# A masked softmax over compressed keys: sixteen small passes on the vector engine made into four wide ones

## The reference, cut to what matters

```python
valid_c = cmp_end[None, :] <= t[:, None]          # cmp_end = 16*c + 31
s_c = einsum('bqgrd,bcgd->bgrqc', qb, k_cmp) * scale + dense_bias(t[:, None] - cmp_end[None, :])
p_c = softmax(where(valid_c, s_c, NEG)) * any(valid_c)
o_c = einsum('bgrqc,bcgd->bqgrd', p_c, v_cmp)      # added with its gate to the other two branches
```

## Time and profile before

| | us |
|---|---|
| median of 3 runs | 2486.55 (2485.26 to 2487.08) |
| the profiled execution | 2487.18 |
| its span on the core | 2485.4 |
| around the span | 1.8 |
| PE busy | 2435.1 |
| DVE busy | 1407.3 |
| ACT busy | 974.9 |
| POOL busy | 177.5 |

### The profile page before, as it was taken

How to read it: one execution, slowest core, us unless ns; L and a number is a source line. 1 busy time by engine, 2 the same in 40 slices (tenths; PEclk the granted TensorE clock), 3 DMA queues, 4 the chain that set the end, 5 groups by cost and what they waited for, 6 DMA issues and landing times.

```text
span 2485.4 us, 31282 instructions
## 1 busy us (share of the span) xinstructions
PE 2435.1 (98%) x12006; PEld 2033.1 (82%) x12006; DVE 1407.3 (57%) x2914; ACT 974.9 (39%) x1808; POOL 177.5 (7%) x245
## 2 busy tenths in 40 slices
PE   9999999999999989999999999999999998999998
PEld 7888889888887878778888888878878887888887
DVE  6435456676666676675443446667644566643444
ACT  4223234432335565553222234555423345422232
POOL 0000000101002221220000000222200002000000
PEclk9999999999999999999999999999999999999999
DMA  4454443233321111113223234211112431223222
GB/s 152 110 130 132 105 138 125 98 107 110 102 85 52 60 52 60 52 60 102 93 92 107 94 102 126 70 58 53 59 63 92 135 119 68 93 83 110 96 86 92
DMA packets 86382, 231.36 MB, mean 93 GB/s; under 512 B 8489, under 2 KB 23465, under 8 KB 86235
## 3 DMA queue, kind: packets, MB, share of 16 engines
q1 hardware_dynamic: 81072, 221.42, 27.2%
q10 hardware_dynamic: 5162, 7.95, 2.1%
HBM read 217.79 MB, written 11.53 MB: 92 GB/s over the span
## 4 chain that ended last, share of the span: by engine, by line
PE 90%; DVE 5%; ACT 3%; issue 2%; DMA 0%; POOL 0%; DVEq 0%; SPq 0%; ACTq 0%
PE bank L975 88%; PE bank L1188 1%; ACT t_pp L1634 1%; DVE t_pp L2142 1%; DVE t_PS L1894 0%; ACT t_whi L1481 0%; ACT t_tmp L1481 0%; ACT t_PS L1481 0%; DVE t_wlo L1889 0%; ACT t_pw L1634 0%; PE bank L1362 0%; DVE t_pw L2142 0%; DVE t_ST L2409 0%; DVE t_CB L2006 0%; DVE t_QS L2235 0%
## 5 line engine op out<-in xcount | busy, mean ns | idle before, releaser
L975 PE MATMUL bank<-t_XH,t_whi 128*128 128x512 f32 x2064 | 813.5, 394 | 6.5 <-DVE t_sa L2142 3.5
L975 PE MATMUL bank<-t_XH,t_wlo 128*128 128x512 f32 x2064 | 804.7, 390 | 0.0
L975 PE MATMUL bank<-t_XL,t_whi 128*128 128x512 f32 x2064 | 804.3, 390 | 0.0
L1889 DVE TENSOR_TENSOR t_wlo<-t_raw,t_whi 128x1024 fp32r<-128x1024 f32 (+2 forms) x418 | 479.4, 1149 | 363.1 <-ACT t_whi L1481 360.1
L1481 ACT ACTIVATE t_whi<-t_raw 128x1024 fp32r<-128x1024 f32 (+3 forms) x422 | 415.7, 988 | 416.8 <-PE bank L975 363.4
L975 PEld LDWEIGHTS bank<-t_XH,t_whi 128*128 128x128 f32 x2064 | 388.2, 188 | 89.5 <-DVE t_sa L2142 4.7
L975 PEld LDWEIGHTS bank<-t_XH,t_wlo 128*128 128x128 f32 x2064 | 387.9, 188 | 82.1
L975 PEld LDWEIGHTS bank<-t_XL,t_whi 128*128 128x128 f32 x2064 | 388.4, 188 | 77.2
L975 PE MATMUL bank<-t_RX,t_whi 128*128 128x512 f32 x1056 | 325.1, 389 | 0.0
L2006 DVE TENSOR_TENSOR t_tmp<-bank,t_RB 128x512 f32<-128x512 f32 x178 | 122.5, 688 | 222.6 <-PE bank L975 217.5
L975 PEld LDWEIGHTS bank<-t_RX,t_whi 128*128 128x128 f32 x1056 | 198.2, 188 | 41.1
(11 more groups left out here) (322 smaller groups left out, 2747.5 us busy)
## 6 DMA issues: line engine op xcount, KB each, us to landing
t_raw<-in_f_in SPq DMA_DIRECT2D x86, 512.0 KB, 3.2
t_raw<-in_f_out SPq DMA_DIRECT2D x32, 384.0 KB, 3.0
t_raw<-in_w_conv SPq DMA_DIRECT2D x24, 512.0 KB, 3.2
t_raw<-in_w_merge SPq DMA_DIRECT2D x24, 512.0 KB, 3.2
t_raw<-in_fg SPq DMA_DIRECT2D x22, 512.0 KB, 3.2
t_raw<-in_fu SPq DMA_DIRECT2D x22, 512.0 KB, 3.2
t_raw<-in_f_out SPq DMA_DIRECT2D x32, 320.0 KB, 3.0
t_raw<-in_w_g SPq DMA_DIRECT2D x16, 512.0 KB, 3.2
```

The source lines that it names most:

```text
L975: return e.matmul(o, l, r, start=start, stop=stop, skip_group_check=True)
L1889: e.tensor_tensor(wlo[n % NRAW][:, 0:width], raw[n % NRAW][:, 0:width], f32(whi[n % NHI][:, 0:width]), ALU.subtract).then_inc(*w_lo.tick(n))
```

## The change

The mask moves to ACT: its copy of cscore's bank becomes four instructions, one per token block, of the function Identity with a bias that is a column of the constants: 1e30 on the partitions (keys) past that block's last key. The table is added in the bank, in place, still block by block; minimum, subtraction, exponential, sum, reciprocal, gate and product are then made once per group for all 16 pairs of block and head by 32 keys. The bank is now freed by the subtraction. POOL's one clearing of t_PC falls away.

```diff
-C_ID, C_INV, C_SEL, C_C1024, C_C256, C_ANY, C_END = 0, 128, 256, 258, 259, 260, 261
+C_ID, C_INV, C_SEL, C_C1024, C_C256, C_ANY, C_LATE, C_END = 0, 128, 256, 258, 259, 260, 261, 265
+    for i in range(4):
+        c[:, C_LATE + i] = np.where(np.arange(P) % 32 >= 8 * i + 7, BIG, 0.0)
...
-                     (2, 0): {0: one("cnorm", g, 0), 1: one("cnorm", g, 1), 2: one("cnorm", g, 2), 3: one("cnorm", g, 3)},
+                     (2, 0): {0: one("cnorm", g, 0), 1: one("cnorm", g, 1), 2: one("cnorm", g, 2)},
...
(ACT)
-            copy(T[4], banks[("cscore", g)]).then_inc(*copied.tick(("ct", g), ("free", ("cscore", g))))
+            for i in range(4):
+                c = slice(i * P, (i + 1) * P)
+                e.activation(T[4][:, c], banks[("cscore", g)][:, c], ACT.Identity, bias=cst[:, C_LATE + i:C_LATE + i + 1]).then_inc(
+                    *copied.tick(("ct", g), ("free", ("cscore", g))))
 
         def csoft(g, i):
-            n = 8 * i + 7
-            sc = T[4][:, i * P:i * P + 4 * n]
-            on.wait_ge(*calc.at(("csub", g, i)))
-            e.activation(sc, sc, ACT.Exp, scale=-1.0).then_inc(*curve.tick(("cexp", g, i)))
+            if i == 3:
+                on.wait_ge(*calc.at(("csub", g)))
+                e.activation(T[4], T[4], ACT.Exp, scale=-1.0).then_inc(*curve.tick(("cexp", g)))
...
(DVE, csoft)
-            e.tensor_tensor(sc, ps, TB4[:, :, c0:c0 + 16 * (n - 1) + 1:16], ALU.add).then_inc(
-                    *evac.tick(("cs", g, i), ("free", ("cback", g))))
-            on.wait_ge(*evac.at(("cs", g, i)))
-            e.tensor_reduce(csm[:, i, 0, :], sc, AX.X, ALU.min).then_inc(*calc.tick(("cmin", g, i)))
-            on.wait_ge(*calc.at(("cmin", g, i)))
-            e.tensor_tensor(sc, sc, csm[:, i, 0, :].unsqueeze(2).to_broadcast([P, 4, n]), ALU.subtract).then_inc(
-                *calc.tick(("csub", g, i)))
+            e.tensor_tensor(ps, ps, TB4[:, :, c0:c0 + 16 * (n - 1) + 1:16], ALU.add).then_inc(*evac.tick(("cs", g, i)))
+            if i == 3:
+                on.wait_ge(*evac.at(("cs", g, 3)))
+                e.tensor_reduce(csum(0), heads16(banks[("cback", g)]), AX.X, ALU.min).then_inc(*calc.tick(("cmin", g)))
+                on.wait_ge(*calc.at(("cmin", g)))
+                e.tensor_tensor(heads16(T[4]), heads16(banks[("cback", g)]), csum(0).unsqueeze(2).to_broadcast([P, 16, 32]),
+                                ALU.subtract).then_inc(*calc.tick(("csub", g), ("free", ("cback", g))))
...
(DVE, cnorm: reduce, reciprocal, gate and product per block i before; now)
+            if i == 0:
+                on.wait_ge(*curve.at(("cexp", g)))
+                e.tensor_reduce(csum(1), heads16(T[4]), AX.X, ALU.add).then_inc(*calc.tick(("csum", g)))
+            if i == 1:
+                on.wait_ge(*calc.at(("csum", g)))
+                e.reciprocal(csum(2), csum(1)).then_inc(*calc.tick(("crec", g)))
...
+                e.tensor_tensor(csm[:, 3, :, :], csm[:, 2, :, :], gn[:, :, 12 * g:12 * g + 12:3], ALU.mult).then_inc(
+                    *calc.tick(("cgate", g)))
+            if i == 2:
...
+                e.tensor_tensor(heads16(PC.rearrange("p i c -> p (i c)")), heads16(T[4]), csum(3).unsqueeze(2).to_broadcast([P, 16, 32]),
+                                ALU.mult).then_inc(*calc.tick(("pcw", g)))
...
(POOL, sparsezero)
-            e.memset(f32(VC[1]), 0.0)
-            e.memset(PC, 0.0).then_inc(*cleared.tick("sparse"))
+            e.memset(f32(VC[1]), 0.0).then_inc(*cleared.tick("sparse"))
```

More of the change, by code:

```diff
@@ L2279, in svs, with heads16, csum @@
                     low_scaled(lo, src, norm_r(1)[0][:, i:i + 1], hi, ("sv", half, i), ("free", ("sv", half, i)))
-        def cpart(i):
-            return 8 * i + 7, T[4][:, i * P:i * P + 4 * (8 * i + 7)].rearrange("p (r c) -> p r c", r=4)
+        def heads16(x):
+            return x.rearrange("p (h c) -> p h c", h=16)
+        def csum(k):
+            return csm[:, k, :, :].rearrange("p i r -> p (i r)")
         def csoft(g, i):
-            n, sc = cpart(i)
+            n = 8 * i + 7
             if i == 0:
@@ L2300, in cnorm @@
-        def cnorm(g, i):
-            n, sc = cpart(i)
-            on.wait_ge(*curve.at(("cexp", g, i)))
-            e.tensor_reduce(csm[:, i, 1, :], sc, AX.X, ALU.add).then_inc(*calc.tick(("csum", g, i)))
-            on.wait_ge(*calc.at(("csum", g, i)))
-            e.reciprocal(csm[:, i, 2, :], csm[:, i, 1, :]).then_inc(*calc.tick(("crec", g, i)))
-            on.wait_ge(*calc.at(("gn",)))
-            on.wait_ge(*calc.at(("crec", g, i)))
-            e.tensor_tensor(csm[:, i, 3, :], csm[:, i, 2, :], gn[:, i, 12 * g:12 * g + 12:3], ALU.mult).then_inc(
-                *calc.tick(("cgate", g, i)))
-            on.wait_ge(*cleared.at("sparse"))
-            if g:
-                on.wait_ge(*full.at(("cturn", g - 1)))
-            on.wait_ge(*calc.at(("cgate", g, i)))
-            e.tensor_tensor(PC[:, i, :].rearrange("p (r c) -> p r c", r=4)[:, :, 0:n], sc,
-                            csm[:, i, 3, :].unsqueeze(2).to_broadcast([P, 4, n]), ALU.mult).then_inc(*calc.tick(("pcw", g)))
+            e.tensor_tensor(ps, ps, TB4[:, :, c0:c0 + 16 * (n - 1) + 1:16], ALU.add).then_inc(*evac.tick(("cs", g, i)))
@@ new lines, in csoft @@
+            if i == 3:
[4 more added lines that the diff above has]
+                                ALU.subtract).then_inc(*calc.tick(("csub", g), ("free", ("cback", g))))
+        def cnorm(g, i):
+            if i == 0:
[4 more added lines that the diff above has]
+                e.reciprocal(csum(2), csum(1)).then_inc(*calc.tick(("crec", g)))
+                on.wait_ge(*calc.at(("gn",)))
+                on.wait_ge(*calc.at(("crec", g)))
+                e.tensor_tensor(csm[:, 3, :, :], csm[:, 2, :, :], gn[:, :, 12 * g:12 * g + 12:3], ALU.mult).then_inc(
+                    *calc.tick(("cgate", g)))
+            if i == 2:
+                on.wait_ge(*cleared.at("sparse"))
+                if g:
+                    on.wait_ge(*full.at(("cturn", g - 1)))
+                on.wait_ge(*calc.at(("cgate", g)))
+                e.tensor_tensor(heads16(PC.rearrange("p i c -> p (i c)")), heads16(T[4]), csum(3).unsqueeze(2).to_broadcast([P, 16, 32]),
+                                ALU.mult).then_inc(*calc.tick(("pcw", g)))
```

## The result

The changed kernel takes 2480.18 us (median of 16 runs, 2478.63 to 2482.25) against 2486.01 us for the kernel before (16 runs, 2483.14 to 2489.09). The ratio is 0.9976, with an interval of 0.997 to 0.9983: 5.8 us less, between 4.2 and 7.5. The kernel is faster, and the difference is clear of the noise, where the forecast gave 0.77 to no change that can be told.

What follows compares the result with a forecast made beforehand. PE, busy 98% of the span, was taken as the bound, so only its waits on DVE or ACT could return. Terms +1.2 - 3.2 + 0.5 - 0.2 - 0.9 - 0.2 = -2.8 us gave 2483.7 us, range 2480.2 to 2487.0.

Steps and rivals of the forecast that it cites:

- the cover given to cnorm: cnorm blocks 1 and 2: hidden by `values` and dense items, nothing gained; block 0 -0.2, block 3 of group 3 -0.9.
- The mask: ACT's four copies before cback add 0.59 us each time, fully paid in groups 0 and 3; sum +1.2 us.
- csoft, blocks 0 and 1: DVE work ahead of `weigh` shrinks: groups 0 to 3 give -1.2, -0.5, -1.0, -0.5; sum -3.2 us.
- block 3: Wide minimum and subtraction add 0.9 us ahead of `weigh` of tile 3, paid only in group 2: +0.5 us.
- `weigh` of tile 3: Group 1, cnorm's head: this `weigh` comes earlier by what DVE gained, an estimated -0.2 us.
- still heads before PE takes it: The held bank, freed 1.4 us later by the change, would still be free heads before PE needs it.
- A dense item gives DVE 5.4 us to catch up, so whatever it does under one is free: Under dense items, 756 to 1084 us: DVE work costs nothing; only small items ahead of `weigh` are paid for.
- In the csoft heads no wait of PE over 0.3 us: Expected sign: no longer PE waits there, except about half a microsecond after block 3 of group 2.
- 1.4 us lost: Group 0: cscore's eight matmuls took 3.50 us at low clock against group 3's 2.08; nothing put in the sum.
- Rival 3: ACT reloads its table around each cscore: 8 loads, 10.3 us, giving +7.5 us, 2494; chance 0.03.
- Rival 1: Gain hidden or paid back, since shorter `weigh` waits uncover `rest`: about 0, 2486 to 2487 us; chance 0.16.
- Rival 2: DVE's catching up dissolves more of PE's `weigh` waits: -5 to -8 us, 2478.5 to 2481.5; chance 0.19.

Runs made afterwards that it cites:

- no mask: Changed kernel with ACT's four masked copies as one plain copy of 512 columns, mask left out; 2477.84 us, ratio 0.9962.
- csoft only: Changed kernel with cnorm block by block as in the kernel before; 2485.9 us, ratio 0.9994.
- bank held: Changed kernel with cback's bank returned to PE's ring two tiles later, at cnorm 2 instead of cnorm 0; 2482.28 us, ratio 0.9981.
- extra at tile 1: Changed kernel with a second, identical sum on DVE (0.68 us) at tile 1 of head (2,0), in all four groups; 2483.81 us, one execution.
- late cback: Changed kernel with cback one tile later and the adds of blocks 0 and 1 sharing tile 1; 2477.39 us, ratio 0.996.
- cnorm only: Kernel before with the wide cnorm alone, csoft per block on a 32-column grid, no mask; 2482.55 us, ratio 0.9984.
- late adds: late cback with block 1's add moved to tile 2 beside block 2's; 2476.24 us, ratio 0.9959.
- late minimum: late cback with minimum, subtraction and exponential moved to tile 0 of head (2,0) and cnorm's three steps one tile later; 2482.41 us, ratio 0.9984.
- before again: Kernel before, unchanged, one more profiled execution; 2489.03 us.

## Why the prediction was wrong, step by step

The step that failed is the cover given to cnorm: it put the saving in blocks 1 and 2 at nothing, and all of cnorm in group 2. The runs show 0.95 us in group 2 and 0.4 more than forecast in group 3. The terms one by one:

**The mask, +1.2 us.** Right in size and place: 0.55 in group 3, 0.56 between cscore and cback in group 0, 0.1 together in the others ("no mask").

**csoft, blocks 0 and 1, -3.2, and block 3, +0.5.** In group 1 the forecast had -0.5 and -0.2 for `weigh` of tile 3, and 0.89 came. In group 3 it had -0.5 with the mask's +0.59, and "csoft only" has +0.05: right. In group 0 all terms together were -0.7, and 0.6 to 0.8 came, which can't be told apart from more or less, since group 0 moves by 1.2 to 1.4 us by itself. In group 2 it had -1.0 + 0.5, and -0.95 came: if blocks 0 and 1 gave their 1.0, block 3 gave nothing back. No run separates the two. The statement that the held bank would be free "still heads before PE takes it" was false. PE took it at 981.79 and waited 0.67 us, but "bank held" shows the price of that wait as nothing.

**cnorm.** "Blocks 1 and 2 are covered, by `values` and dense items" is the step that failed. cnorm in group 2 was forecast at 0 and gave 0.95; group 3 was forecast at -1.0 and gave 1.39. In group 2 DVE runs without a pause from csoft to the dense item, so that what is saved in cnorm's tiles arrives at the end as far as PE can follow. In group 3 a dense item does lie behind, but it brings DVE work of its own and waits for ACT, and 0.43 of 0.68 us added before it come out behind it ("extra at tile 1"). "A dense item gives DVE 5.4 us to catch up, so whatever it does under one is free" counted the item's length on PE, and not DVE's share in it.

**What made me take it for covered** was in group 2 PE's list of waits. I took its rows for the sum of what can come back. In group 2 it shows 0.16 us of wait where 0.53 us lie between two starts, against 0.21 when DVE is early, and it fell by 0.3 where 1.87 came back. In group 3 the list did show the waits that went, and the fault was to count the cover as free.

**The signs.** PE's 1.15 us before 1082.78 is gone, as said. "In the csoft heads no wait of PE over 0.3 us" failed: waits of 0.43 to 0.52 us for `rest` (t_PS) are left in groups 0, 2 and 3, and of 0.36 for `weigh` in group 1. PE's wait before cback of group 0 was to be 1.9 and is 3.30; the row of 1.30 from which that came was short because cscore ran slowly.

**The clock.** "1.4 us lost" for the eight matmuls of cscore at the low clock is wrong. Cback starts 5.38 us behind cscore's start with them and 5.37 without: they ran in time that PE would have waited. To put nothing in the sum for the clock was right by these groups, for another reason than given.

**The single operations.** Reduce 691 ns and subtraction 692 (forecast 0.69 each), exponential 632, masked copy 364, as forecast. The add in the bank, for which no row stood before, takes 0.20, 0.25 and 0.38 us at 28, 60 and 124 columns in after's timeline, where before it took 0.19, 0.24 and up to 0.367: +0.01, taken as nothing. The Trainium skill, VectorE: DVE Perf Modes, section "The TRN2 errata", gives instructions of VectorE that read PSUM 62 fixed cycles more than those that read SBUF; by that, 0.065 us each for reduce and subtraction, an estimate from its figures. The traces don't agree: the reduce from the bank takes 691 ns and the reduce of the same shape from SBUF 677.

**The rivals.** Rival 3 fell: no table load stands between 756 and 1084 us in after. Rival 1 fell with the 4.9 us. Rival 2 has the right time and only half the right reason. It let DVE's catching up dissolve the waits for `weigh` of its one row, 7.2 us of them; that row fell by 2.8 us, the one at the transposes by 2.0, and in group 2 most of what came back was never in the list.

**By term.** Forecast -2.8: groups 0 to 3 as -0.7, -0.7, -0.5, -0.9. Measured -4.8 to -4.9: about -0.7, -0.89, -1.87, -1.37. Of the 2 us between them 1.4 are from group 2, 0.95 of these from cnorm's cover and 0.45 from csoft, and 0.4 are cnorm's in group 3. Between 4.9 and the measured 5.8 lies 0.9 us, which the interval covers. In the profiled pair "between" is 0.94 shorter in after; a second pair has 1.5. That is the clock, behind the same stall of 2.50 us: the mean granted clock of "between" is 0.93 where it takes 46.4 to 46.6 us (both executions of before, csoft only, late cback), 0.96 where it takes 45.1 to 45.5 (after, cnorm only, late adds and the rest), and 1.00 in late minimum, which has 43.83. Whether the clock favours the changed kernel there as a rule or by the draw stays open. All three executions with cnorm block by block have the long stretch of low clock, and eight of the ten with the wide cnorm the short one; these are single executions. So part of the measured 5.8 may be luck of the clock; the 4.8 to 4.9 of the groups would give 2481 to 2482 us, inside the range but still 2 us beyond the sum.

## What to carry to other kernels

Before calling a saving hidden, look whether the engine that it falls on has any idle time in brackets between the saved instructions and the supposed cover, and count that engine's own share of the cover. Where it has none, instructions saved come back until the next engine becomes the last; in group 2 an instruction added behind that point was nearly free again. Compare starts of the same instructions in two traces, segment by segment: in this kernel that resolves 0.03 us from one execution, and it sees short waits that the list of waits leaves out, 1.6 of 1.87 us in group 2.

## What the runs showed of the hardware that I had not expected

- A wide reciprocal isn't free of its width: 16 values per partition take 244 ns, against 0.18 us for 4 values and 0.16 for one in the timeline of before. The forecast counted it among "the two small ones" of a tile; it is 0.07 us dearer than a small one.
- A stretch of low clock behind a stall costs 1 to 2 us where PE sets the pace, and nothing where it doesn't. Near 1845 us, some 760 us behind the last of the changed work, PE stands 2.04 us for DVE and then makes 24 matmuls on t_OA. From their first start to the next matmul on t_GQ it takes 7.20 us in after with granted clock 0.76, and 5.57 in "cnorm only" with 1.00 (windows; after first). Where the clock stayed full there, the stretch from the last milestone to the end is 1.2 to 2.3 us shorter (table: "no mask", "cnorm only", "late minimum", "late adds").

```profile
1842.15:1849.35 7.20, 7.20 (x25) 5.76 (x26) 1.95 (x3) 0.00 (x0) 0.00 (x0) 0.76 0.00 1
```

```profile
1844.59:1850.16 5.57, 5.57 (x24) 4.61 (x25) 1.96 (x3) 0.00 (x0) 0.00 (x0) 1.00 0.00 0
```

- Against that stand cscore of group 0 (3.50 us instead of 2.06, cback at the same distance) and group 2 of "before again" (0.50 over 2 us, the group 47.19 against 47.20): PE would have waited in any case.
- DVE writes an f32 bank in place at the speed at which it writes SBUF, to 0.01 us at 28 to 124 columns.
